# A recurrent mixer computed inside its own input product, with its small matmuls on 128 rows

## The chip, the cores and the metric

The kernel runs on one core of one Trainium2 chip (trn2). The metric is the device time of one launch in microseconds (us); the time given for a kernel is the median of its runs.

## The reference, cut to what matters

Two transformer blocks run one after the other over 256 tokens of width 1024, in float32; the first adds 16 meta tokens in front (272 columns). The first layer of the first block, the one the change is about, is a gated linear recurrence ("hgrn2") between a normalisation and an output product:

```python
hn = rmsnorm(h, g[0])
q, f_pre, i, g = split(hn @ w_in, 4)            # w_in: 1024 x 4096
f = lb + (1 - lb) * sigmoid(f_pre); logf = log(f); k = 1 - f      # 8 heads of 128
# per head, in chunks: the 16 meta tokens, then 4 chunks of 64
b = cumsum(logf); q_in = q*exp(b); k_in = k*exp(-b); k_out = k*exp(b_last - b)
o = tril(q_in @ k_in.T) @ v + q_in @ S          # S: state at the chunk's start
S = exp(b_last) * S + k_out.T @ v
o = rmsnorm_per_head(o) * head_gain * silu(g);  mix = o @ w_out
```

After it come its feed-forward layer, an attention layer ("fox") with its own, and the second block: a gated delta rule, a feed-forward layer, a latent attention ("mla") and a feed-forward layer. The second block scales, shifts and gates with `mod = silu(c) @ ada_w + ada_b`, 96 columns of 128 values, which depends on no token.

## The kernel before, in words

Activations lie feature-major: 8 tiles of 128 features by 272 (or 256) columns. Every weight product is computed to float32 precision with three fp32r matmuls per 128x128 block: high part of w by high part of x, high by low, low by high (L355 to L357). Weights stream through one ring of four slots. An item is normally 16 blocks (1 MB, two output tiles of eight blocks each, 48 matmuls). SP loads it into `raw` seven items ahead, once a slot is free. ACT copies it to `w_hi` (`split_hi`, L210), and DVE takes `w_lo` = raw - w_hi (`split_lo`, L214), three items ahead of PE. `STREAM` is the order of the items, `each` and `steps` the loops over them. ACT takes the finished tiles out of PSUM. The stages lie in blocks (`run`, `nc.Block`); at the end of each the engines wait for each other.

Some products are hosts of the modulation: beside an item, SP loads 1 MB of `ada` into a room of two slots (`mod_load`, L190), and DVE multiplies by the row `c_row` and sums (`mod_column`, L196, two of them, then L203). `MOD_HOSTS` says which product takes how many of the 48 modulation items, and `modulation_scales` turns the scales of a layer into gains in a block of its own once they are complete.

The first layer goes so. (1) Entry (`NormEntry`): ACT squares (L505), PE sums over features (L580), ACT takes the root (L509), DVE inverts (L530), scales (L567) and makes the low half (L545), ACT the high half (L519). After its entry ACT splits items 1 and 2 and applies Silu to `c_row` (L806). (2) Product `a_in`: 16 items in the order q, f, v, g of 4 items each, copied to `qfig` (L824). It hosts 8 modulation items, one at every second item. (3) `hgrn2`, in a block of its own. ACT and DVE first prepare all heads: the lower bounds `lb`, Sigmoid on f (L1425), f and k (L1485, L1488), Ln (L1428), scans (L1493). Then they go head by head (L1432 to L1437 on ACT, L1499 to L1511 on DVE). PE starts when the first head's k_out is there. Per head it has 6 transposes (L1542, L1543), 3 scores (L1545, two instructions each, as every float32 matmul here), 4 additions to the state (L1554 for the 16 meta rows, L1557 with 64 rows each), and for the head before, the output: 3 matmuls with the masked scores (L1525) and 4 with the states (L1529). Between them ACT copies the transposes (L1417, L1418) and takes the output out (L1412), and DVE masks the scores (L1452, L1454) and steps the state (L1460, L1464). (4) Product `a_out`, whose entry (`HeadNormEntry`) starts with squares on ACT (L605) after the block's end.

The attention layer of the same block (`Fox`) already has the form of a product with the heads woven in: its tile matmuls are L981 to L983, its head matmuls L998 to L1043.

Of the kernel before, what the change touches and what calls it, by code (L numbers as in the profile page):

```python
# [23 lines left out]
P = 128  # L24
# [36 lines left out]
STREAM = ([("a_in", 16, 16), ("a_out", 4, 16), ("up0", 22, 16), ("down0", 16, 11)]  # L61
# [8 lines left out]
for _g in range(4):  # L70
    SOURCE |= {f"fox_q{_g}": ("b_q", _g), f"fox_k{_g}": ("kv", _g), f"fox_v{_g}": ("kv", 4 + _g)}
# [3 lines left out]
for _name, _n, _every in (("a_in", 16, 2), ("a_out", 4, 1), ("down0", 16, 2), ("b_out", 4, 1),  # L75
                          ("down1", 16, 2), ("gdn_gate", 4, 1), ("dn0", 16, 2), ("mla_out", 4, 1)):
    MOD_HOSTS[_name] = (_at, _every)
    _at += _n // _every
# [20 lines left out]
def fused_model(nc, w, params_d, consts_d, hT_d, c_d, pos_d, out_d):  # L99
    with ExitStack() as ctx:  # L100
# [132 lines left out]
        class Product:  # L233
# [3 lines left out]
            def __init__(self, name, tiles, k_tiles, x_hi, x_lo, cols, act_out=None, dve_out=None, pool_out=None,  # L237
# [11 lines left out]
                hosts = n // every if every else 0  # L249
# [8 lines left out]
                def mod_at(s, turn):  # L258

                    slot = (s - first) % SLOTS // every % 2  # L260
                    i = turn * (SLOTS // every) + (s - first) // every
                    turns = turn * (SLOTS // every // 2) + (s - first - every * slot) // (2 * every)
                    return i + mod_first, slot, turns + turns0[slot]

                def sync(sp):
# [16 lines left out]
                    if first == 0:  # L282
                        for r in range(SLOTS, ahead):
                            load(sp, name, r, r % SLOTS)
# [371 lines left out]
        with nc.Block() as block:  # L656
            @block.sync
            def _(sp):
# [3 lines left out]
                for r in range(LEAD):  # L662
                    load(sp, "a_in", r, r % SLOTS)
                sp.dma_start(c_row[:, :], c_d).then_inc(c_in.sem, 16)
                load(sp, "a_in", LEAD, LEAD)
# [13 lines left out]
        def modulation_scales(layer):  # L679

            with nc.Block() as block:
                @block.vector
                def _(dve):
                    for part, gains in ((1, "norm_mix"), (4, "norm_ffn")):
                        dve.scalar_tensor_tensor(mod[:, layer, part, :], mod[:, layer, part, :], 1.0,
                                                 par(gains, layer * KD, KD), ALU.add, ALU.mult)
# [107 lines left out]
        with ExitStack() as outer:  # L794
            qfig = sbuf(outer, "qfig", [P, 4 * KD, T1])
            with ExitStack() as phase:
                x_hi, x_lo = sbuf(phase, "x_hi_a", [P, KD, T1], F32R), sbuf(phase, "x_lo_a", [P, KD, T1], F32R)

                def first_high(act):
                    split_hi(act, 0, 0, 0, starts["a_in"][2])  # L800

                def high_then(act):
                    for r in range(1, LEAD):
                        split_hi(act, r, r, 0, starts["a_in"][2])
                    act.wait_ge(c_in.sem, 16)
                    act.activation(c_row[:, :], c_row[:, :], ACT.Silu).then_inc(c_ready.sem, 1)  # L806

                def first_low(dve):
                    dve.wait_ge(params_in.sem, 16)
                    split_lo(dve, 0, 0, 0, starts["a_in"][2])  # L810

                def low_then(dve):
                    for r in range(1, LEAD):
                        split_lo(dve, r, r, 0, starts["a_in"][2])
                    dve.wait_ge(c_ready.sem, 1)
# [3 lines left out]
                def a_in_out(act, j, s, where):  # L819
                    item_ready(act, "a_in", j)  # L820
                    for t in range(2):
                        at = j * 2 + t
                        d = qfig[:, at, :] if isinstance(at, int) else qfig[:, bass.ds(at, 1), :]
                        last = act.activation(d, where(t)[:, 0:T1], ACT.Copy)  # L824
                    last.then_inc(item_out.sem, 1)
                product("a_in", 2, KD, x_hi, x_lo, (0, T1), act_out=a_in_out, entry=entry)

            q, f, v, g = (qfig[:, i * KD:(i + 1) * KD, :] for i in range(4))
            hgrn2(nc, sbuf, sig, bank, q, f, v, g, work, par, con, ident)
# [444 lines left out]
        modulation_scales(0)  # L1274
# [27 lines left out]
        modulation_scales(1)  # L1302


        with ExitStack() as outer:
# [33 lines left out]
            with ExitStack() as phase:  # L1339
# [3 lines left out]
                        entry=entry, sqrt_next=True)  # L1343
        ffn_layer(1, real, modcol(1, 4), "gu1", "dn1", (modcol(1, 2), False), 0, shift=modcol(1, 3))
# [24 lines left out]


def hgrn2(nc, sbuf, sig, bank, q, f, v, g, k, par, con, ident):

    real = (META, T1)
    tiles = [(0, META), (META, P), (META + P, P)]
    n_chunks = SEQ // 64
    with ExitStack() as scope:
        b = sbuf(scope, "log_decay", [P, HEADS, T1])
        e = sbuf(scope, "decay", [P, HEADS, T1])  # L1380
        k_in = sbuf(scope, "k_in", [P, HEADS, T1])
        lb = sbuf(scope, "lower_bound", [P, 6, KD])
        lb_max, lb_exp, lb_done = sig("lb_max"), sig("lb_exp"), sig("lb_done")
        sigmoided, silued = sig("f_sigmoided"), sig("g_silued")
        f_made, k_made, logged, summed = sig("f_made"), sig("k_made"), sig("f_logged"), sig("b_summed")
        exped, q_in, k_in_made, diffed = sig("b_exped"), sig("q_in"), sig("k_in_made"), sig("b_diffed")
        diff_exped = sig("diff_exped")
        reset = con("reset_hgrn")
        v_tok = sbuf(scope, "v_tok_a", [P, 2, 3, P])
        k_tok = sbuf(scope, "k_tok_a", [P, 2, 3, P])  # L1390
        attn = sbuf(scope, "attn_a", [P, 2, 3, P])
        state = sbuf(scope, "state_a", [P, 2, n_chunks, P])
        turned, copied, masked = sig("turned"), sig("tok_copied"), sig("attn_masked")
        ds_done, stated, o_done, o_out = sig("ds_done"), sig("stated"), sig("o_done"), sig("o_out")

        def added_to(y, c):


            return bank[y][:, 3 * P:4 * P] if c == 2 else bank[6][:, c * P:(c + 1) * P]

        k_out_made = sig("k_out_made")
        behind = 4

        with nc.Block() as block:
            @block.scalar
            def _(act):
                def take_out(i):
                    if i >= 2:  # L1410
                        act.wait_ge(o_done.sem, o_done.at(i - 1))
                        act.activation(v[:, i - 2, :], bank[7][:, 0:T1], ACT.Copy).then_inc(o_out.sem, 1)  # L1412
                    if i < HEADS:
                        y = i % 2
                        act.wait_ge(turned.sem, turned.at(i + 1))
                        for src, dst in ((bank[2 + y], v_tok), (bank[4 + y], k_tok)):
                            act.activation(dst[0:META, y, 0, :], src[0:META, 0:P], ACT.Copy)  # L1417
                            last = act.activation(dst[:, y, 1:3, :],  # L1418
                                                  src[:, P:3 * P].rearrange("p (x c) -> p x c", x=2), ACT.Copy)
                        last.then_inc(copied.sem, 1)  # L1420

                act.wait_ge(lb_max.sem, lb_max.at(3))
# [924 lines left out]
```

## Time and profile before

| | us |
|---|---|
| median of 3 runs | 1754.86 |
| lowest and highest run | 1753.28, 1766.72 |
| the profiled execution | 1766.81 |
| its span (first to last instruction) | 1765.0 |
| busy in the span: PE / DVE / ACT / POOL | 1554.9 / 1020.3 / 803.8 / 221.0 |
| mean granted TensorE clock | 0.912 |

A granted clock of 1.00 is 2.4 GHz and 0.50 is 1.2 GHz. A duration of a PE instruction holds its passage through the array and overlaps with the next one's; the pace is read from one start to the next. A row of the timeline gives start, length, engine, line, operation, output and inputs, and in brackets how long the engine sat idle before it and what released it. A row of the windows gives the busy time and the number of instructions of each engine in a stretch, then the granted clock, the share of the DMA engines and GB/s.

### The profile page before, as it was taken

The numbers are of one execution on the slowest core, as the hardware profiler recorded it, in microseconds if no ns is written. First come the engines' busy times: TensorE is split into PE (matmuls) and PEld (weight loads), VectorE is DVE, ScalarE is ACT, GpSimd is POOL, SyncE is SP. The second block draws the span as 40 slices with busy tenths as digits, with TensorE's granted clock in tenths as the row PEclk, the third lists the DMA queues.
The fourth block names the chain that finished last, engine by engine and source line by source line (L and its number), as shares of the span: only waits on it lengthen the run. The fifth ranks groups of instructions, "written<-read, shape, count | busy, mean of one in ns | idle before, by whom it ended". The sixth has DMA issues, their size and how long they took to land. (4 is left out here: it accounts for less than half of the span.)

```text
span 1765.0 us, 29368 instructions
## 1 busy us (share of the span) xinstructions
PE 1554.9 (88%) x11429; PEld 1475.3 (84%) x11429; DVE 1020.3 (58%) x1663; ACT 803.8 (46%) x1372; POOL 221.0 (13%) x341
## 2 busy tenths in 40 slices
PE   6976879999887998999979768979999677989997
PEld 5975678999876777999969758979999576779997
DVE  5565176776765447777778652245447634664443
ACT  5453354544454453555445472364434434543332
POOL 0000101211044320112000006211210000001200
PEclk9995599999998898999989987989999786889999
DMA  8840142548622233455925700024549332335451
GB/s 331 306 174 1 41 151 96 177 151 302 241 98 95 71 113 127 167 190 197 352 97 189 252 22 1 1 96 144 187 142 355 123 108 95 149 125 182 159 167 54
DMA packets 41134, 265.97 MB, mean 151 GB/s; under 512 B 4560, under 2 KB 5712, under 8 KB 15312
## 3 DMA queue, kind: packets, MB, share of 16 engines
q1 hardware_dynamic: 41040, 264.72, 41.8%
q8 instruction: 59, 0.97, 0.2%
q14 instruction: 35, 0.29, 0.0%
HBM read 263.65 MB, written 1.05 MB: 150 GB/s over the span
## 5 line engine op out<-in xcount | busy, mean ns | idle before, releaser
L214 DVE TENSOR_TENSOR w_lo<-raw,w_hi 128x2048 fp32r<-128x2048 f32 (+3 forms) x224 | 466.1, 2083 | 289.2 <-ACT w_hi L210 286.6
L210 ACT ACTIVATE w_hi<-raw 128x2048 fp32r<-128x2048 f32 (+3 forms) x224 | 387.6, 1732 | 56.5 <-PE bank L357 50.9
L355 PE MATMUL bank<-x_hi_up,w_hi 128*128 128x272 f32 (+1 forms) x704 | 203.7, 289 | 8.2 <-DVE x_lo_up L545 8.1
L355 PE MATMUL bank<-x_hi_gu,w_hi 128*128 128x256 f32 x704 | 202.0, 287 | 8.5 <-DVE x_lo_gu L543 8.4
L357 PE MATMUL bank<-x_hi_up,w_lo 128*128 128x272 f32 (+1 forms) x704 | 202.2, 287 | 0.0
L356 PE MATMUL bank<-x_lo_up,w_hi 128*128 128x272 f32 (+1 forms) x704 | 201.7, 287 | 0.0
L356 PE MATMUL bank<-x_lo_gu,w_hi 128*128 128x256 f32 x704 | 200.8, 285 | 0.0
L357 PE MATMUL bank<-x_hi_gu,w_lo 128*128 128x256 f32 x704 | 199.0, 283 | 0.0
L355 PEld LDWEIGHTS bank<-x_hi_gu,w_hi 128*128 128x128 f32 x704 | 133.8, 190 | 10.4 <-issue 8.9
L355 PEld LDWEIGHTS bank<-x_hi_up,w_hi 128*128 128x128 f32 x704 | 133.7, 190 | 9.9 <-issue 8.8
L357 PEld LDWEIGHTS bank<-x_hi_gu,w_lo 128*128 128x128 f32 x704 | 135.5, 192 | 0.0
L356 PEld LDWEIGHTS bank<-x_lo_gu,w_hi 128*128 128x128 f32 x704 | 134.6, 191 | 0.0
L356 PEld LDWEIGHTS bank<-x_lo_up,w_hi 128*128 128x128 f32 x704 | 134.1, 191 | 0.0
L357 PEld LDWEIGHTS bank<-x_hi_up,w_lo 128*128 128x128 f32 x704 | 133.9, 190 | 0.0
L355 PE MATMUL bank<-a_hi_up,w_hi 128*128 128x272 f32 (+1 forms) x352 | 102.8, 292 | 0.0
L580 PE MATMUL bank<-work,constants 128*128 128x256 f32 (+2 forms) x154 | 54.5, 525 | 52.8 <-ACT work L505 52.7
L357 PE MATMUL bank<-a_hi_up,w_lo 128*128 128x272 f32 (+1 forms) x352 | 100.2, 285 | 0.0
L356 PE MATMUL bank<-a_lo_up,w_hi 128*128 128x272 f32 (+1 forms) x352 | 100.1, 284 | 0.0
L356 PE MATMUL bank<-a_lo_gu,w_hi 128*128 128x256 f32 x352 | 98.3, 279 | 0.0
L355 PE MATMUL bank<-a_hi_gu,w_hi 128*128 128x256 f32 x352 | 98.3, 279 | 0.0
L357 PE MATMUL bank<-a_hi_gu,w_lo 128*128 128x256 f32 x352 | 98.3, 279 | 0.0
L580 PEld LDWEIGHTS bank<-work,constants 128*128 128x128 f32 x154 | 39.3, 265 | 66.0 <-ACT work L505 57.6
(393 smaller groups left out, 3942.2 us busy)
## 6 DMA issues: line engine op xcount, KB each, us to landing
raw<-w_up SPq DMA_DIRECT2D x44, 1024.0 KB, 4.9
raw<-w_gu SPq DMA_DIRECT2D x44, 1024.0 KB, 4.9
raw<-w_down SPq DMA_DIRECT2D x32, 704.0 KB, 5.3
raw<-w_dn SPq DMA_DIRECT2D x32, 704.0 KB, 4.1
raw<-w_a_in SPq DMA_DIRECT2D x16, 1024.0 KB, 6.8
mod_w_down<-w_ada SPq DMA_DIRECT2D x16, 1024.0 KB, 7.1
raw<-w_gdn_qkv SPq DMA_DIRECT2D x12, 1024.0 KB, 5.0
mod_w_a_in<-w_ada SPq DMA_DIRECT2D x8, 1024.0 KB, 6.5
```

What stands on the lines that cost most here:

```text
L210: act.activation(w_hi[:, s, 0:blocks * P], raw[:, s, 0:blocks * P], ACT.Copy).then_inc(hi_split.sem, 1)
L214: dve.tensor_tensor(w_lo[:, s, 0:blocks * P], raw[:, s, 0:blocks * P], w_hi[:, s, 0:blocks * P].bitcast(F32), ALU.subtract).then_inc(lo_sp ...
L355: pe.matmul(o, w_hi[:, s, b], x_hi[:, xk, cols[0]:cols[1]], start=begin, stop=False)
L356: pe.matmul(o, w_hi[:, s, b], x_lo[:, xk, cols[0]:cols[1]], start=False, stop=False)
L357: last = pe.matmul(o, w_lo[:, s, b], x_hi[:, xk, cols[0]:cols[1]], start=False, stop=end)
L580: last = pe.matmul(bank[6][:, 0:c1 - c0], ones, work[:, k, c0:c1], start=k == 0, stop=k == n - 1)
```

## The change

`hgrn2` and product `a_in` become one class, `Hgrn`, run in one block with an order written out by hand:

- The items of `a_in` come in the order f0 to f3, then q0 v0 q1 v1 q2 v2 q3 v3, then g0 to g3. Tiles alternate between banks 0 and 1, and `half_done` and `copied_out` count single tiles.
- The lower bounds are made ahead of the entry (ACT's Exp ahead of the squares). ACT splits items 1, 2 and 3 after the entry, and not `c_row`, whose Silu moves behind the heads.
- Order: 8 tiles of f (ACT applies Sigmoid as it takes them out, DVE makes f and k), all logarithms, 2 tiles of q, then twelve steps `head(i)`, each followed by one item (two tiles) for i from 0 to 10. In `head(i)` PE makes the output of head i-4, transposes and scores of head i-2, and the additions to the state of head i-3.
- The scratch tiles `b`, `e`, `k_in` hold 3 heads in place of 8; chunk decays are kept in a small tile. Transposed keys go into four tiles of 128 rows of which the rest is zero, and the meta rows of v and of the scores are padded with zeros to 128 rows. POOL clears them once. So L1554 and L1557 become 4 matmuls of 128 rows, and the meta matmul of L1525 contracts over 128 rows.
- Modulation: `a_in` hosts none; `gdn_out` (4), `mla_in` (1) and `uq` (3) become hosts. `modulation_scales(1)` is split in two, with a further block after `mla_out`.

```diff
-STREAM = ([("a_in", 16, 16), ("a_out", 4, 16), ...
+A_ITEMS = [f"a_f{g}" for g in range(4)] + [f"a_{x}{g}" for g in range(4) for x in "qv"] + [f"a_g{g}" for g in range(4)]
+STREAM = ([(name, 1, 16) for name in A_ITEMS] + [("a_out", 4, 16), ...
-for _name, _n, _every in (("a_in", 16, 2), ("a_out", 4, 1), ("down0", 16, 2), ("b_out", 4, 1),
-                          ("down1", 16, 2), ("gdn_gate", 4, 1), ("dn0", 16, 2), ("mla_out", 4, 1)):
+for _name, _n, _every in (("a_out", 4, 1), ("down0", 16, 2), ("b_out", 4, 1), ("down1", 16, 2), ("gdn_gate", 4, 1),
+                          ("gdn_out", 4, 1), ("dn0", 16, 2), ("mla_in", 3, 4), ("uq", 3, 1), ("mla_out", 4, 1)):
...
+                order = [tile("f", n) for n in range(KD)] + [("logs", "", 0), tile("q", 0), tile("q", 1)]
+                items = [(x, m) for m in range(4) for x in "qv"][1:] + [("g", m) for m in range(4)]
+                for i in range(HEADS + 4):
+                    order.append(("head", "", i))
+                    if i < len(items):
+                        x, m = items[i]
+                        order += [tile(x, 2 * m), tile(x, 2 * m + 1)]
+                    if i == HEADS:
+                        order.append(("gates", "", 0))
...
+                    def product_tile(event):
+                        r, t = ring_of(event), event[2] % 2
+                        s, m = r % SLOTS, turn[event]
+                        if t == 0:
+                            pe.wait_ge(lo_split.sem, r + 1)
+                        if m >= 2:
+                            tile_taken(pe, in_turn[m - 2])
...
+                        if 2 <= i < HEADS + 2:
+                            j, y = i - 2, i % 2
+                            tile_taken(pe, tile("v", j))
+                            pe.wait_ge(q_in.sem, q_in.at(j + 1))
+                            pe.wait_ge(k_in_made.sem, k_in_made.at(j + 1))
+                            pe.wait_ge(k_out_made.sem, k_out_made.at(j + 1))
...
+                            for c in range(n_chunks):
+                                last = pe.matmul(bank[6][:, c * P:(c + 1) * P], k_tok[:, y, c, :],
+                                                 v_tok[:, y, (c + 1) // 2, :], start=True, stop=True)
...
+                def gpsimd(pool):
+                    pool.memset(k_tok[:, :, :, :], 0.0)
+                    pool.memset(v_tok[:, :, 0, :], 0.0)
+                    pool.memset(attn[:, :, 0, :], 0.0).then_inc(cleared.sem, 1)
...
-        modulation_scales(1)
+        modulation_scales(1, [(1, "norm_mix")])
...
+        modulation_scales(1, [(4, "norm_ffn")])
```

On DVE, `head(i)` does in this order: the state of head i-3, the mask of head i-2, the scan of head i+1, q_in and k_out of head i-1, then the chunk decays, k_in and the differences of head i; `split_lo` of the item four further on comes after each second tile. On ACT it is: two Exps of head i, the Exp for k_out of head i-1, the output of head i-4, the five copies of head i-2; then the two tiles and `split_hi`.

## Rows read from the trace of the kernel before

**Rows 1.** Windows: product `a_in`, preparation, head by head, entry of `a_out`.

```profile
22.75:122.00 99.25, 99.20 (x768) 98.74 (x768) 65.39 (x71) 47.63 (x57) 0.00 (x0) 0.97 0.72 264
122.00:139.70 17.70, 0.00 (x0) 0.00 (x0) 12.64 (x41) 14.88 (x33) 0.00 (x0) 0.64 0.13 53
139.70:213.60 73.90, 61.14 (x272) 51.76 (x272) 25.01 (x79) 18.34 (x57) 0.00 (x0) 0.52 0.00 1
213.60:225.50 11.90, 5.87 (x16) 4.27 (x16) 1.75 (x5) 11.53 (x27) 5.79 (x8) 0.76 0.45 177
```

**Rows 2.** Timeline of PE: one head of `hgrn2`, clock 0.50.

```profile
165.99 1.72 PE L1525 MATMUL bank<-attn_a,v_tok_a 16*128 16x16 f32 x6 [1.58 <-issue]
...
169.11 0.42 PE L1542 MATMUL bank<-constants,qfig 128*16 128x128 f32 x1
...
170.52 1.39 PE L1545 MATMUL bank<-qfig,k_in 128*16 128x16 f32 x6
171.84 0.79 PE L1554 MATMUL bank<-v_tok_a,k_tok_a 16*128 16x128 f32 x2
...
175.37 1.73 PE L1525 MATMUL bank<-attn_a,v_tok_a 16*128 16x16 f32 x6 [1.58 <-issue]
```

**Rows 3.** Timeline of ACT: last output of `hgrn2`, then the entry of `a_out`.

```profile
213.63 0.40 ACT L1412 ACTIVATE qfig<-bank 128x272 f32<-128x272 f32 x1 [5.84 <-PE bank L1529]
...
214.86 2.67 ACT L605 ACTIVATE qfig<-qfig 128x272 f32<-128x272 f32 x8 [0.28 <-PEq L1406]
```

**Rows 4.** Timeline of ACT: after the entry of `a_in`, and the logarithms.

```profile
27.21 3.70 ACT L210 ACTIVATE w_hi<-raw 128x2048 fp32r<-128x2048 f32 x2
30.93 1.28 ACT L806 ACT_TABLE_LOAD   x1
...
129.75 2.67 ACT L1428 ACTIVATE qfig<-qfig 128x272 f32<-128x272 f32 x8
```

**Rows 5.** Timeline of DVE: first splits of `a_in`.

```profile
29.14 4.50 DVE L214 TENSOR_TENSOR w_lo<-raw,w_hi 128x2048 fp32r<-128x2048 f32 x2 [1.36 <-ACT w_hi L210]
```

**Rows 6.** Timeline of PE: `a_in` starts after a gap.

```profile
22.75 0.56 PE L355 MATMUL bank<-x_hi_a,w_hi 128*128 128x272 f32 x1 [4.03 <-DVE x_lo_a L545]
...
28.50 0.29 PE L355 MATMUL bank<-x_hi_a,w_hi 128*128 128x272 f32 x1
```

**Rows 7.** Timeline of PE: delta rule, float32 matmuls at clock 1.00.

```profile
1110.46 1.92 PE L2035 MATMUL bank<-constants,inverse 128*128 128x128 f32 x16
1112.22 3.68 PE L2022 MATMUL bank<-inverse,coupling_level 128*128 128x64 f32 x32
```

**Rows 8.** Windows: three of the woven attention, one of the delta rule.

```profile
602.00:604.00 2.00, 1.01 (x9) 0.79 (x7) 2.00 (x8) 0.00 (x0) 1.81 (x4) 1.00 0.36 61
...
606.00:608.00 2.00, 2.00 (x10) 1.30 (x10) 1.31 (x6) 0.23 (x1) 0.16 (x1) 0.50 0.35 147
...
612.00:614.00 2.00, 2.00 (x18) 2.00 (x17) 0.00 (x0) 0.00 (x0) 0.00 (x0) 1.00 0.00 0
...
1078.00:1080.00 2.00, 2.00 (x11) 2.00 (x11) 0.42 (x1) 0.00 (x0) 0.00 (x0) 0.50 0.00 0
```

**Rows 9.** Timeline of DVE: end of `uq`, end of `gdn_out`, last item of `mla_out`.

```profile
1446.85 1.23 DVE L214 TENSOR_TENSOR w_lo<-raw,w_hi 128x1024 fp32r<-128x1024 f32 x1 [3.04 <-ACT w_hi L210]
...
1179.17 2.29 DVE L214 TENSOR_TENSOR w_lo<-raw,w_hi 128x2048 fp32r<-128x2048 f32 x1 [3.41 <-ACT w_hi L210]
1183.35 3.26 DVE L557 SCALAR_TENSOR_TENSOR h<-work,mod,h 128x256 f32<-128x256 f32 x8 [1.88 <-PEq L398]
...
1546.08 1.22 DVE L196 CUSTOM_DVE_ANT_0 mod_w_mla_out<-mod_w_mla_out,c_row 128x1024 f32<-128x1024 f32 x1
...
1548.96 3.25 DVE L557 SCALAR_TENSOR_TENSOR h<-work,mod,h 128x256 f32<-128x256 f32 x8 [0.31 <-PEq L398]
```

**Rows 10.** Timeline of ACT: first instruction after `uq`.

```profile
1450.42 0.72 ACT L505 ACTIVATE work<-latent 128x256 f32<-128x256 f32 x2 [0.28 <-PEq L398]
```

More of the change, by code:

```diff
@@ L58 @@
 NCONST = _at
-STREAM = ([("a_in", 16, 16), ("a_out", 4, 16), ("up0", 22, 16), ("down0", 16, 11)]
+A_ITEMS = [f"a_f{g}" for g in range(4)] + [f"a_{x}{g}" for g in range(4) for x in "qv"] + [f"a_g{g}" for g in range(4)]
+STREAM = ([(name, 1, 16) for name in A_ITEMS] + [("a_out", 4, 16), ("up0", 22, 16), ("down0", 16, 11)]
           + [(f"fox_q{g}", 1, 16) for g in range(4)] + [("fox_gate", 1, 8)]
@@ L248, in __init__ @@
                 mod_first, every = MOD_HOSTS.get(name, (0, 0))
-                hosts = n // every if every else 0
+                hosts = -(-n // every) if every else 0
                 ahead = LEAD + SLOTS
@@ L258, in mod_at @@
                 def mod_at(s, turn):
+                    if hosts == 1:
+                        return mod_first, 0, turns0[0]
                     slot = (s - first) % SLOTS // every % 2
@@ L281, in sync @@
                         mod_load(sp, room, mod_first + i, i)
-                    if first == 0:
-                        for r in range(SLOTS, ahead):
-                            load(sp, name, r, r % SLOTS)
                     cut = max(first, first + n - ahead)
@@ L662, in _ @@
                 for r in range(LEAD):
-                    load(sp, "a_in", r, r % SLOTS)
+                    load(sp, A_ITEMS[r], r, r % SLOTS)
                 sp.dma_start(c_row[:, :], c_d).then_inc(c_in.sem, 16)
-                load(sp, "a_in", LEAD, LEAD)
+                load(sp, A_ITEMS[LEAD], LEAD, LEAD)
             @block.vector
@@ L677, in _, with modulation_scales @@
                 pe.wait_ge(consts_in.sem, 16)
-        def modulation_scales(layer):
+        def modulation_scales(layer, parts):
             with nc.Block() as block:
@@ L683, in _ @@
                 def _(dve):
-                    for part, gains in ((1, "norm_mix"), (4, "norm_ffn")):
+                    for part, gains in parts:
                         dve.scalar_tensor_tensor(mod[:, layer, part, :], mod[:, layer, part, :], 1.0,
@@ L794, in fused_model @@
         with ExitStack() as outer:
             qfig = sbuf(outer, "qfig", [P, 4 * KD, T1])
+            q, f, v, g = (qfig[:, i * KD:(i + 1) * KD, :] for i in range(4))
             with ExitStack() as phase:
                 x_hi, x_lo = sbuf(phase, "x_hi_a", [P, KD, T1], F32R), sbuf(phase, "x_lo_a", [P, KD, T1], F32R)
[L799 to L815, printed above, removed]
-                entry = NormEntry(lambda k: h[:, k, :], KD, (0, T1), gain1(0, 0), x_hi, x_lo, act_first=first_high,
-                                  dve_first=first_low, act_then=high_then, dve_then=low_then)
@@ L819, in a_in_out @@
[L819 to L828, printed above, removed]
@@ L829, in fused_model @@
-            hgrn2(nc, sbuf, sig, bank, q, f, v, g, work, par, con, ident)
+                run(Hgrn(phase, x_hi, x_lo, q, f, v, g))
             with ExitStack() as phase:
```

439 lines of the change are left out of this document (257 added, 182 removed).

## The prediction, as it was written before the run

> **What bounds the kernel now.** I read the windows by stage first, then the timelines of PE, ACT and DVE inside the first layer, then the clock of other stages. In product `a_in` PE is busy 99.20 of 99.25 us [rows 1]: PE is the bound, DVE has 34 us and ACT 52 us to spare. In the next 17.7 us PE does nothing while ACT and DVE prepare the heads. Then come 73.9 us of heads in which PE is busy 61.1, but at a clock of 0.52, that is nearly always at 1.2 GHz [rows 1]. One head takes 175.37 - 165.99 = 9.38 us, of which PE waits 1.58 for the states and works 7.80 [rows 2]. So 91.6 us pass between the product and the end of the heads (122.0 to 213.6) whose work for PE, at full clock, is small. The entry of `a_out` starts with squares at 214.86 [rows 3]; this moment is what I compare.
>
> **PE's work per head at full clock.** The trace shows no such head. In the delta rule float32 instructions of the same kind run at 1.00: 16 with 128 columns in 1112.22 - 1110.46 = 1.76 us, 0.11 each, and 32 with 64 columns in about 3.5 (3.68 less the 0.2 in which the last one ends), 0.11 too [rows 7]. A head after the change has 6 transposes (0.66), 4 score instructions of 128 columns and 2 small ones (0.5), 8 for the state (0.88), 6 for the masked scores (0.66) and 8 for the output from the states (0.88): 3.6 us. The other way, half of the 7.80 measured at 1.2 GHz is 3.9. I take 3.85, as switches between operands and semaphores come on top of the 3.6. Ends: 3.6 (-2 us over 8 heads) and 7.8, if the heads ran at 1.2 GHz (+32 us).
>
> **Padding.** It changes 8 instructions of the state's additions and 2 of the output. At 1.2 GHz the two of L1554 take 0.79 us with only 16 rows; two of 128 rows would take 0.22 and 0.42, the length of the transpose at 169.11 [rows 2], so fewer rows buy no time. I take nothing. Ends: 8 x 8 x 0.11 = 7 us gained or lost if an instruction of part rows cost double or were free. The zeroing by POOL runs at the start, where POOL has no other work, and its first reader comes some 50 us later. The Trainium skill (TensorE: Matmul & The Clock Gate, Part 3, packing small matmuls) says that matmuls in different row groups run side by side; that speaks against padding, since L1557's 64-row pieces alternate between two halves. By it the padding costs at most half of 6 x 0.11 us a head, 2.6 us in all. The measured 0.79 us for the two 16-row ones shows that at least those gained nothing.
>
> **The start of the new block.** The lower bounds and their Exp come ahead of the squares: +0.2 us. PE's first tile is done at 28.50 + 0.2 [rows 6], the second at 31.75. The third needs bank 0, which ACT takes only after three splits. ACT ends x_hi at 27.2, splits until 27.4 + 5.5 = 32.9 (3.70 for two, [rows 4]), loads the Sigmoid table (1.28, as at L806), takes tile 0 at 34.2 to 34.6. DVE's splits (4.50 for two, [rows 5]) are ready before. So PE idles 2.9 us, where it now idles none, and may restart at 1.2 GHz. After the 4.03 us gap at 22.75 the first 24 matmuls took 28.50 - 22.75 = 5.75 us, against (122.0 - 28.5) / 31 = 3.02 us for each later tile [rows 1, 6]. The same after 2.9 us costs up to 2.7; I take 1.5. Six more tiles of f: 34.65 + 1.5 + 18.1 = 54.2. PE goes on with the two tiles of q until 60.2. ACT meanwhile takes f7 (54.6), splits (56.5), loads a table and makes the 8 logarithms (1.28 + 2.67, [rows 4]: 60.5), and takes q0 at 60.85. PE waits 0.7 and starts v0 at 60.9; v0 and v1 end at 66.9.
>
> **The woven part.** From there PE has 10 items (20 x 3.02 = 60.3) and 8 heads (8 x 3.85 = 30.8): 158.0, then ACT's copy of the last output (0.40) and the block's end (0.28, both [rows 3]): squares at 158.7. The wait of 1.58 per head goes, since the states have a whole item's time to be made. What is late next? One period is 6.04 + 3.85 = 9.9 us. DVE's head work is (12.64 + 25.01) / 8 = 4.7 us and ACT's, tables included, (14.88 + 18.34) / 8 = 4.2 [rows 1]; the splits add 2.3 and 1.9, the copies of two tiles 0.7 on ACT. DVE is busy 7.0 and ACT 6.8 of 9.9. The tightest order is DVE's: after the second tile's end ACT copies and splits (2.3), DVE makes w_lo (2.3), then the head: states, mask, scan, q_in, k_out, about 3.5; k_out is out 8.1 us after the tile, and PE reads it at 9.9 plus the output matmuls. Nothing is late by this, with 1.8 us to spare. For hand-overs that come out less well, twelve of them, I add 2 us. Saved in the stage: 214.86 - 158.7 - 2 = 54 us.
>
> In `a_in` DVE loses 8 modulation items and SP their loads (8 MB of DMA). DVE was no bound there, so this gains nothing. The ring's loads go through the same seven-item lead; an item has 10 us in the weave where it had 6.
>
> **The modulation's new hosts.** `gdn_out`: the last `split_lo` begins at 1179.17, the next stage's DVE work at 1183.35, 4.18 later. In `mla_out`, a host, the last `mod_column` runs from 1546.08 and the next stage starts at 1548.96, 2.88 later, to which the split's 2.2 is added: 5.1 [rows 9]. So +0.9. `uq`: last split at 1446.85, ACT goes on at 1450.42 [rows 9, 10]; with 1.2 + 2.88 it would be 1450.95: +0.5. `mla_in` has its column beside the first item, where DVE waits for ACT: nothing. The further block: one small operation between two barriers of 0.3: +0.6. Sum +2; ends 0 and 6, if a modulation item lands late in `uq` (three items in 16 us, where SP must issue the third after the first is used).
>
> **Sum.** -54 + 2 = -52 us. The profiled execution took 1766.81, 1.81 more than its span, so it becomes 1715. It is the slowest of the three runs; 52 us off the median give 1754.86 - 52 = 1703.
>
> **Rivals.** (A) The clock falls at every head. For it: 61 us of float32 work at 0.52 [rows 1], and a window of the delta rule with PE busy 2.00 of 2.00 at 0.50 [rows 8], so busy float32 matmuls do not by themselves bring 2.4 GHz. Against it: in the woven attention the clock stood at 1.00 over a window with PE only half busy, fell to 0.50 in the next four us, and was back at 1.00 by 612, after a few us of tile matmuls [rows 8]. Price: 3.9 more per head and 1.6 on the tiles behind it, 8 x 5.5 = 44 us: 1747. The Trainium skill (the same page, Part 4, transposes) says that transposes do not count as work for the clock gate; by it A gains weight. The heads' rows at 0.52 agree with it, but each head here has only 0.66 us of transposes between 6 us of products.
>
> (B) The hand-overs, not PE, set the period: DVE, last in the ring from `split_hi` over `split_lo` to k_out, has 1.8 us to spare, and decides from there on. If a period is 12 instead of 9.9 us, 8 x 2.1 = 17 us: 1720. For it: both engines work in strict order, with five waits on DVE per head. Against it: their busy sums of 7 us.
>
> (C) The slower side: the clock stays at 1.2 GHz from the first head on, since head work stands in each stretch. Then 60.3 + 30.8 us take twice as long, +91: 1794. It decides if the tiles between two heads do not bring the clock back. Against it: `a_in` regained 2.4 GHz at 28.5 after 5.75 us of them [rows 6].
>
> (D) The padding doesn't do what it is there for, and changes nothing. That moves no number above.
>
> **How the numbers follow.** My forecast 0.80, B 0.11, A 0.06, C 0.03. A measurement of this kernel tells about 1% (17.5 us) from no change. Forecast and B are faster by more: 0.91; A lies within: 0.06; C is slower: 0.03. The range: down to 1690 (3.6 per head, no slow restart, late hand-overs none, and runs that differ by 13 us), up to 1726 (B, or the clock falling at three heads in ten).
>
> **What would show it.** The first squares of `a_out`'s entry near 159 to 162; the clock 0.9 or more in the weave; no matmul row with 64 or 16 rows in it; PE's gap of about 3 us after its second tile and 0.7 us before v0; head groups of 3.9 us between pairs of 3.0 us tiles; `gdn_out` and `uq` ending about 1 us later. I am wrong if PE's waits in the weave add up to over 10 us, or if head groups take 7 us.

## The result, and the profile after

| | before | after |
|---|---|---|
| median (lowest to highest), runs | 1754.45 us (1753.28 to 1766.72), 4 | 1714.07 us (1712.86 to 1715.16), 4 |
| profiled execution: time, span | 1766.81, 1765.0 | 1712.86, 1711.0 |
| TensorE clock over the span | 0.912 | 0.928 |
| first squares of the entry of `a_out` | 214.86 | 159.44 |
| first product matmul of `mla_out` | 1524.0 | 1470.7 |

The ratio is 0.9759 (95% interval 0.972 to 0.9799): 40.4 us off the median, where the forecast was 52 off (1703). The range (1690 to 1726) holds it. Profile against profile the gain is 1766.81 - 1712.86 = 53.95. So the two comparisons differ by 13.5 us, and explaining that is most of what follows.

First the stage that was changed. The windows of the kernel after (from the first product tiles on; columns as in [rows 1]):

```profile
22.00:28.00 6.00, 5.94 (x29) 5.14 (x29) 4.72 (x13) 4.20 (x7) 0.00 (x0) 0.72 0.17 68
28.00:32.00 4.00, 2.57 (x21) 2.34 (x19) 3.77 (x2) 3.98 (x4) 0.00 (x0) 1.00 0.15 18
32.00:40.00 8.00, 6.36 (x28) 6.39 (x29) 6.50 (x8) 3.97 (x5) 0.00 (x0) 0.57 0.99 389
40.00:50.00 10.00, 10.00 (x82) 10.00 (x81) 4.99 (x9) 3.88 (x5) 0.00 (x0) 1.00 0.40 147
60.00:70.00 10.00, 9.36 (x75) 9.17 (x74) 3.89 (x7) 7.98 (x13) 0.00 (x0) 1.00 0.60 211
100.00:110.00 10.00, 10.00 (x87) 9.78 (x85) 6.10 (x14) 5.08 (x13) 0.00 (x0) 1.00 0.30 107
150.00:158.00 8.00, 8.00 (x69) 8.00 (x68) 3.54 (x5) 2.06 (x4) 0.00 (x0) 1.00 0.38 131
```

Where [rows 1] had 17.7 us without PE and then 73.9 us at a clock of 0.52, PE is now busy nearly all the time, and at a clock of 1.00 from 40 us to the end of the block. The exceptions are the two that were forecast: one gap with a restart (28 to 40), and one wait of 0.64 us ahead of the first tile of v, at 61.34. Behind that PE waits for nothing until the squares.

One head in the woven order, timeline of PE (start, us, engine, line, operation, tiles, count). Up to 109.14 the tile matmuls of the item before it run; from 112.90 those of the next:

```profile
109.14 0.83 PE L894 MATMUL bank<-attn_a,v_tok_a 128*128 128x16 f32 x6
109.81 1.00 PE L898 MATMUL bank<-qfig,state_a 128*128 128x64 f32 x8
110.65 0.49 PE L912 MATMUL bank<-constants,qfig 128*16 128x128 f32 x3
110.98 0.49 PE L914 MATMUL bank<-constants,qfig 128*16 128x128 f32 x3
111.40 0.86 PE L916 MATMUL bank<-qfig,k_in 128*16 128x16 f32 x6
112.09 1.06 PE L925 MATMUL bank<-v_tok_a,k_tok_a 128*128 128x128 f32 x8
112.90 0.38 PE L881 MATMUL bank<-x_hi_a,w_hi 128*128 128x272 f32 x1
...
119.01 0.83 PE L894 MATMUL bank<-attn_a,v_tok_a 128*128 128x16 f32 x6
```

The six lines answer to [rows 2]. They take 112.90 - 109.14 = 3.76 us where a head took 7.80 and a wait of 1.58. Not one of them waits for another engine, and the period is 119.01 - 109.14 = 9.87 us.

The two places where the change costs something, timelines of ACT and PE after the entry of `a_in` (the bracket is the idle time and what ended it), and the end of the stage on ACT, which answers to [rows 3]:

```profile
26.29 5.50 ACT L212 ACTIVATE w_hi<-raw 128x2048 fp32r<-128x2048 f32 x3
31.81 1.28 ACT L1065 ACT_TABLE_LOAD   x1
33.10 0.69 ACT L1065 ACTIVATE qfig<-bank 128x272 f32<-128x272 f32 x2
...
158.75 0.40 ACT L1039 ACTIVATE qfig<-bank 128x272 f32<-128x272 f32 x1 [1.11 <-PE bank L898]
159.44 2.67 ACT L606 ACTIVATE qfig<-qfig 128x272 f32<-128x272 f32 x8 [0.28 <-PEq L399]
```
```profile
33.65 0.56 PE L881 MATMUL bank<-x_hi_a,w_hi 128*128 128x272 f32 x1 [3.08 <-ACT qfig L1065]
```

PE's third tile waits for ACT, which first finishes three splits (5.50) and a table load (1.28). The gap is 3.08 us. After it the first 26 matmuls take 39.67 - 33.65 = 6.02 us, and at 0.125 each they would have taken 3.25: the restart costs 2.8 in this profile. The cost isn't the same in every profile, as the part on the prediction shows.

The stage ends 214.86 - 159.44 = 55.4 us earlier. The rest of the kernel gives 1.5 of that back up to the end, by the two profiles. But one stage of it, the latent attention (scores at L1335 and L1336 before, L1611 and L1612 after), does not stand still, as the experiments show.

### The profile page after: what moved, and what is told of

Read it like the earlier page. It is cut to its first block and busy times, and to the rows that moved or that the text cites. A ratio compares the mean times of both kernels' runs of the same rounds, so it can differ in the third digit from the quotient of the medians.

```text
span 1711.0 us, 29323 instructions
## 1 busy us (share of the span) xinstructions
PE 1527.9 (89%) x11429; PEld 1456.7 (85%) x11429; DVE 1019.8 (60%) x1671; ACT 798.1 (47%) x1367; POOL 222.3 (13%) x344
## 3 DMA queue, kind: packets, MB, share of 16 engines
HBM read 263.65 MB, written 1.05 MB: 155 GB/s over the span
```

## The experiments

Three questions were open: what the two other parts of the change (new hosts, padding) do alone, why before has two groups of times, and which of them the profile of before belongs to. Of the 55 later runs of before, beside which the experiments were measured in three batches, 50 lie at 1752 to 1757 us and 5 at 1767 to 1769: 4 of the 23 in the first batch, 1 of the 23 in the second, none of the 9 in the third. The first batch ran beside the first four experiments, the second beside the four with padded scores or the early take, the third beside the last three; each was on another chip of the same type.

**The kernel before once more.**

> The kernel before, unchanged, for a second profile. The profiled executions differ by 54 us (1766.8 to 1712.9), the medians by 40. Theory: the first profiled execution was slow in the head-by-head stretch, where the clock stood at 0.52; in the others part of it runs at 2.4 GHz. Then this profile takes about 1754, its entry of a_out starts with squares near 203 instead of 214.9, and the clock of the heads is 0.6 or more. Rival: that stretch is the same (squares at 214 to 215, clock 0.52) and the 13 us lie in later stages, which differ from run to run.

Measured: 1755.42. My theory put the difference into the heads; it fell. The squares are at 211.78 (214.86 in the first profile), so the heads were 3.1 us shorter, but most of the 11.4 us between the two profiles isn't there: the later stages level that out (the first matmul of the latent attention's stage starts at 1473.7 in the one and 1474.5 in the other), and then `mla_out` starts at 1524.0 and at 1513.8. Between the two points lies the latent attention. Its scores, with 128 rows (L1335) and 64 rows (L1336), in the profile given for the kernel before (duration in ns least/median/most, then first to last start):

```profile
L1335 PE MATMUL bank<-k_nope,q_mla x32: 275/452/793, 1485.2 to 1515.9; 128*128 128x128 f32 x16, 128*128 128x256 f32 x16
L1336 PE MATMUL bank<-latent,q_mla x32: 272/530/793, 1485.9 to 1516.5; 64*128 64x128 f32 x16, 64*128 64x256 f32 x16
```

The same two lines of the same kernel in this run:

```profile
L1335 PE MATMUL bank<-k_nope,q_mla x32: 275/378/483, 1485.7 to 1505.7; 128*128 128x128 f32 x16, 128*128 128x256 f32 x16
L1336 PE MATMUL bank<-latent,q_mla x32: 272/374/480, 1486.1 to 1506.3; 64*128 64x128 f32 x16, 64*128 64x256 f32 x16
```

One kernel, two courses: 31 us of scores with matmuls of up to 0.79 us, or 20 us with at most 0.48. The window of four us in the middle of it, in the first profile of before and in this one:

```profile
1492.00:1496.00 4.00, 4.00 (x10) 2.01 (x9) 1.77 (x8) 0.91 (x4) 0.00 (x0) 0.50 0.00 0
```
```profile
1492.00:1496.00 4.00, 4.00 (x23) 2.77 (x22) 3.10 (x15) 1.51 (x8) 0.00 (x0) 1.00 0.00 0
```

PE is busy 4.00 of 4.00 in both, once at 0.50 with 10 matmuls, once at 1.00 with 23. The profile from which I predicted is of the longer course; the median of before is of the shorter one. And after? Its own lines:

```profile
L1611 PE MATMUL bank<-k_nope,q_mla x32: 275/421/793, 1433.6 to 1462.6; 128*128 128x128 f32 x16, 128*128 128x256 f32 x16
L1612 PE MATMUL bank<-latent,q_mla x32: 272/480/792, 1434.0 to 1463.2; 64*128 64x128 f32 x16, 64*128 64x256 f32 x16
```

After has the longer course (29 us of scores) in its profile, and its other three runs lie within 2.3 us of that one; that they ran the same course is read from their times.

**Only the new hosts**, with `a_in` and `hgrn2` as before:

```diff
-for _name, _n, _every in (("a_in", 16, 2), ("a_out", 4, 1), ...
+for _name, _n, _every in (("a_out", 4, 1), ... ("gdn_out", 4, 1), ("dn0", 16, 2), ("mla_in", 3, 4), ("uq", 3, 1), ...
...
-                hosts = n // every if every else 0
+                hosts = -(-n // every) if every else 0
...
-        modulation_scales(1)
+        modulation_scales(1, [(1, "norm_mix")])
...
+        modulation_scales(1, [(4, "norm_ffn")])
```

> The kernel before with only the modulation moved: a_in hosts none, gdn_out, mla_in and uq do, and the gains of the second layer's feed-forward are made in a further block. My sum says +2 us (0.9 in gdn_out, 0.5 in uq, 0.6 for the block). Rival: the eight items in a_in did hold DVE or the loads back, then it is faster than before by some us; or a late item in uq, then +4 to +6.

Measured: 1766.97 (1757.9 to 1770.99, 12 runs), ratio 1.0055 (1.0032 to 1.0079). That is 12.7 more than before, and 11 of the 12 runs lie at 1764 to 1771. The profile has the scores from 1486.5 to 1517.8, again with up to 0.79 us for one. So the small rearrangement of DVE's work seems to take the attention to its longer course in nearly every run (by their times; one run has a profile). What it costs by itself is measured further down.

**Only the padding**, in the unwoven `hgrn2`:

```diff
-        k_tok = sbuf(scope, "k_tok_a", [P, 2, 3, P])
+        k_tok = sbuf(scope, "k_tok_a", [P, 2, n_chunks, P])
...
-                            pe.matmul(bank[7][:, t0:t0 + n], v_tok[0:n, y, x, :], attn[0:n, y, x, 0:n],
+                            pe.matmul(bank[7][:, t0:t0 + n], v_tok[:, y, x, :], attn[:, y, x, 0:n],
...
-                            last = pe.matmul(added_to(y, c + 1), k_tok[r, y, 1 + c // 2, :],
-                                             v_tok[r, y, 1 + c // 2, :], start=True, stop=True)
+                            last = pe.matmul(added_to(y, c), k_tok[:, y, c, :],
+                                             v_tok[:, y, (c + 1) // 2, :], start=True, stop=True)
```

> The kernel before with only the padding: transposed keys, meta values and meta scores on 128 rows in the unwoven heads. My theory: padding alone changes nothing (+-3 us), the heads stay near 0.52 and 9.4 us each. Rival: the matmuls of 16 and 64 rows are what keeps the clock at 1.2 GHz in the heads; then the heads run at 2.4 GHz, 5.5 us each in place of 9.4, and the kernel is some 20 to 30 us faster.

Measured: 1741.82 (1732.98 to 1752.78, 12 runs), ratio 0.9933 (0.9904 to 0.9963), 12.5 less than before, and the squares at 198.73 in place of 211.78. My expectation that the padding changes nothing falls. The runs scatter: two lie at 1733 to 1737, five at 1740 to 1742, five at 1750 to 1753, so 12.5 is the middle of gains from about 2 to 21. Most of the gain in the profile is in the clock. First the heads of before (second profile), then the same stretch and parts of it in this kernel:

```profile
139.70:198.00 58.30, 48.77 (x234) 41.33 (x233) 22.13 (x71) 16.82 (x55) 0.00 (x0) 0.59 0.00 1
```
```profile
139.70:198.00 58.30, 45.08 (x272) 40.29 (x270) 24.70 (x79) 21.33 (x67) 0.00 (x0) 0.73 0.00 1
144.00:153.50 9.50, 6.29 (x54) 5.75 (x54) 7.61 (x25) 4.94 (x18) 0.00 (x0) 1.00 0.01 2
154.30:155.72 1.42, 1.42 (x8) 1.01 (x8) 0.19 (x1) 0.40 (x1) 0.00 (x0) 0.50 0.00 0
161.00:173.50 12.50, 10.92 (x51) 9.76 (x52) 2.26 (x8) 2.45 (x8) 0.00 (x0) 0.50 0.00 1
```

The five profiles with unpadded heads have 0.53 to 0.59 over this stretch, this one 0.73. In both kinds the clock goes up and down; without the padding it is at 1.00 in one to three short stretches, with it in two long ones and two short ones. Which instruction raises it isn't shown: in the padded kernel it also stays at 0.50 through a whole head (161 to 173.5), and without the padding, in the second profile of before, it rises between 160.5 and 161.0, over transposes and before the additions (161.72). (The Trainium skill, TensorE: Matmul & The Clock Gate, Part 4, says that transposes do not count for the clock as other matmuls do. This trace doesn't decide it: the clock has fallen already when the six transposes at 154.30 begin (0.85 from 153.5 to 154.0), while the six at 148.42 run at 1.00; in the weave the same six transposes per head stand between product tiles and the clock stays at 1.00.)

**The weave without the padding.** The first hunk undoes the padding of the keys; the meta matmuls get their 16 rows back the same way. With it go one more semaphore wait ahead of the additions, a third addition into another bank, and one copy less on ACT:

```diff
-                            for c in range(n_chunks):
-                                last = pe.matmul(bank[6][:, c * P:(c + 1) * P], k_tok[:, y, c, :],
-                                                 v_tok[:, y, (c + 1) // 2, :], start=True, stop=True)
+                            pe.wait_ge(masked.sem, masked.at(j + 1))
+                            pe.matmul(added_to(y, 0), k_tok[0:META, y, 0, :], v_tok[0:META, y, 0, :], start=True, stop=True)
+                            for c in range(n_chunks - 1):
+                                r = slice(64 * (c % 2), 64 * (c % 2) + 64)
+                                last = pe.matmul(added_to(y, c + 1), k_tok[r, y, 1 + c // 2, :],
+                                                 v_tok[r, y, 1 + c // 2, :], start=True, stop=True)
```

> The kernel after without the padding: additions to the state with 16 and 64 rows, the third of them in another bank, the meta scores and values with 16 rows, no zeroing. My theory: as the kernel after, 1714 +-3 us, clock 1.00 in the weave. Rival: part rows let the clock fall at each head; then the weave is up to 44 us longer and the kernel is near the one before.

Measured: 1718.09 (1715.55 to 1720.38, 6 runs), 4.0 more than after. The clock over 100 to 120 us is 1.00, so here it isn't the clock. Timeline of PE, one head and the start of the next:

```profile
109.53 0.29 PE L886 MATMUL bank<-x_hi_a,w_lo 128*128 128x272 f32 x1
109.75 1.03 PE L897 MATMUL bank<-attn_a,v_tok_a 16*128 16x16 f32 x6
110.62 1.00 PE L901 MATMUL bank<-qfig,state_a 128*128 128x64 f32 x8
...
112.99 0.48 PE L928 MATMUL bank<-v_tok_a,k_tok_a 16*128 16x128 f32 x2
113.41 0.71 PE L931 MATMUL bank<-v_tok_a,k_tok_a 64*128 64x128 f32 x6
114.04 0.39 PE L884 MATMUL bank<-x_hi_a,w_hi 128*128 128x272 f32 x1
...
120.25 1.03 PE L897 MATMUL bank<-attn_a,v_tok_a 16*128 16x16 f32 x6
```

The period is 10.50 in place of 9.87. The outputs from masked scores, whose first product (of three) has 16 rows, take 110.62 - 109.75 = 0.87 (0.67 with 128 rows), and start 0.22 after the last tile matmul in place of 0.12. That place costs 0.20 + 0.10 = 0.30. The additions take 114.04 - 112.99 = 1.05 (0.81) and start 0.78 after the scores' last line (0.69, that line being the same in both): 0.24 + 0.09 = 0.33. Together that is the 0.63, at full clock, and 8 x 0.63 = 5.0 us in all. The squares are only 4.0 us later than in the kernel after (163.40), since the restart behind PE's gap was cheaper here by 1.4. Of the 0.33 a part may belong to the added wait or the other bank; for the 0.30 there is a run with nothing else changed (the last one below). The Trainium skill has a rule for either side. TensorE: Matmul & The Clock Gate, Part 3, has matmuls in different row groups run side by side; the eight instructions of the additions take longer with part rows here, not less. The Trainium skill's page TensorEngine Tiling (Array Packing), Tiling Modes, Key Properties, says "Changing tiling mode (not just tile) drains the TensorE"; the rows fit that, with 0.30 to 0.33 us for each such place.

**The attention's short scores padded too.** If matmuls of part rows keep the clock down, padding the 64-row scores of the latent attention (L1612) must bring the shorter course for good. The edit, on the kernel after:

```diff
-                    return pe.matmul(out, q_rope[p0:p0 + 64, h_ // 2, q0:q0 + qn], k_rope[p0:p0 + 64, 0, 0:kn],
+                    return pe.matmul(out, q_rope[:, h_ // 2, q0:q0 + qn], k_pad[:, h_ % 2, 0:kn],
...
+                        for y in range(2):
+                            r = slice(64 * y, 64 * y + 64)
+                            last = dve.tensor_tensor(k_pad[r, y, :], x[r, t, :], other[r, i, :], ALU.add)
...
+                pool.memset(k_pad[64:P, 0, :], 0.0)
+                pool.memset(k_pad[0:64, 1, :], 0.0).then_inc(zeroed.sem, 1)
```

> The kernel after, and besides the rotated keys of the latent attention (64 rows per head, in two halves of one tile) in two tiles of 128 rows, the other half zero, so that its logits have no matmul of 64 rows. Theory: that attention has two ways to run, 32 us with the clock at 1.00 and 43 us with it at 0.50; the median of before holds the first, the kernel after always the second, and the part rows are what lets the clock stay low. Then this kernel takes 1714 - 11 = 1703, first logits to the entry of mla_out in 32 us or less. Rival: rows do not matter, only the moment at which the stage begins; then it stays at 1714 or takes either value at random.

Measured: 1700.44 (1699.18 to 1702.06, 5 runs), ratio 0.9685 (0.9659 to 0.9712), 13.6 less than after. The lines of the two scores:

```profile
L1611 PE MATMUL bank<-k_nope,q_mla x32: 273/378/382, 1434.0 to 1450.5; 128*128 128x128 f32 x16, 128*128 128x256 f32 x16
L1612 PE MATMUL bank<-k_rope_padded,q_mla x32: 275/327/379, 1434.3 to 1450.9; 128*128 128x128 f32 x16, 128*128 128x256 f32 x16
```

The scores start 0.3 to 0.4 us later than in the kernel after (1434.0 against 1433.6), and end 12.3 us earlier (1450.9 against 1463.2); no matmul is over 0.38 us.

**The same edit on the kernel before:**

> The kernel before with the same padding of the rotated keys. Theory: its runs near 1767 (4 of 23) go, the rest stays within 2 us of 1753. Rival: no change in how often the slow value comes.

Measured: 1751.79 (1748.91 to 1754.14, 12 runs), ratio 0.9979 (0.9964 to 0.9994). None of the 12 runs is in the upper group, but with only 1 of 23 runs of before there in the same batch, this alone shows little. The scores now take 16.6 us (1486.1 to 1502.7) where the unpadded ones took 20.2 in the second profile of before (1486.1 to 1506.3), whose clock was at 1.00 from 1488 on: an estimate of 3.6 us for what the padding is worth here without a change of course.

**The same edit on the kernel with only the new hosts:**

> The moved modulation alone (as e2, which took 1767) with the padded rotated keys. Theory: the 13 us that e2 lost are 11 of the attention's clock and 2 of the hosts themselves; so this is 2 us above e6. Rival: the hosts cost 10 us or more by themselves (DVE or DMA), then it stays near 1765.

Measured: 1754.38 (1753.08 to 1758.8, 11 runs), ratio 1.0001 (0.9986 to 1.0016). The 12.7 us of the hosts shrink to 1754.38 - 1751.79 = 2.6. That is their own price; the other 10 were the attention's clock. The two hosts kernels ran on different chips, but that isn't the cause: the next kernel, with unpadded scores and on the same chip as this one, has the longer course. And with the attention in one course on both sides, the whole change is 1700.44 - 1751.79 = -51.4 us.

**The third tile's wait.** On the kernel after, ACT takes the first tile out before it splits item 2, and the second before it splits item 3:

```diff
-                    for r in range(1, LEAD + 1):
-                        split_hi(act, r, r, 0, 16)
+                    split_hi(act, 1, 1, 0, 16)
...
+                            if turn[event] < 2:
+                                split_hi(act, n + 2, n + 2, 0, 16)
```

> The kernel after with ACT taking the first tile of f ahead of its splits of items 2 and 3. In the profile of after PE idled 3.1 us there and then ran 6 us at 1.2 GHz. Theory: both go, 3.1 + 2.9 = 6 us, squares of a_out's entry at 153.5. Rival: the restart at 1.2 GHz comes anyway, at another place, then 3 us.

Measured: 1708.2 (1705.61 to 1710.96, 5 runs), ratio 0.9726 (0.9699 to 0.9753), 5.9 less than after. The windows show neither gap nor restart:

```profile
22.00:30.00 8.00, 7.48 (x40) 7.33 (x41) 6.50 (x15) 5.81 (x9) 0.00 (x0) 0.65 0.15 56
30.00:34.00 4.00, 4.00 (x33) 3.79 (x32) 2.77 (x2) 3.99 (x5) 0.00 (x0) 1.00 0.45 125
```

The squares come at 154.30, 5.1 earlier. The gap and the restart had cost 3.1 + 2.8 = 5.9 in the profile of after; PE's first matmul comes 0.7 us later here (22.52 against 21.84). The two profiles as wholes differ by 1.9 us only (1710.96 and 1712.86), because this one has the scores of the attention for 31.3 us (1430.1 to 1461.4) where that of after had 29.6.

**Both edits together.**

> The kernel after with both: padded rotated keys (e5: 1700.4) and the early taking of the first tile of f (e8: 6 us). Theory: they lie in different stages and add: 1694 to 1695. Rival: the moved start puts the attention or another stage at a bad moment for the clock; then 1700 or more.

Measured: 1696.86 (1694.73 to 1697.88, 5 runs), ratio 0.9666 (0.9653 to 0.9679), the fastest kernel here. Over the padded attention alone the early take gives 3.6 us. The squares are 3.9 earlier than there (154.75 against 158.67), where they were 5.1 earlier without the padding. The difference fits the restart: it had cost 2.9 in the profile of after and 1.6 in that of the kernel with the padded attention, so there was less to win.

**The modulation column ahead of the split**, in the last item of a host (on top of both edits), so that the stage's end doesn't wait for the column:

```diff
+                        column_first = host and isinstance(r, int) and r == first + n - 1
+                        if column_first:
+                            mod_column(dve, room, *mod_at(s, turn))
...
```

> As e9, and in the last item of each host with a modulation column per item DVE makes the column ahead of the split. Theory: DVE's end of a_out, b_out, gdn_gate, gdn_out, uq and mla_out comes up to 1 us earlier each, 3 to 5 us in all: 1690. Rival: PE or ACT ends these stages anyway, or the later split is late at the next entry; then no change (+-1 us) against e9.

Measured: 1699.4 (1698.18 to 1702.16, 5 runs), 2.5 slower than without. DVE's timeline at the end of `gdn_out` shows one cause:

```profile
1123.12 1.23 DVE L198 CUSTOM_DVE_ANT_0 mod_w_gdn_out<-mod_w_gdn_out,c_row 128x1024 f32<-128x1024 f32 x1 [2.66 <-DMA mod_w_gdn_out<-w_ada]
...
1125.62 2.28 DVE L216 TENSOR_TENSOR w_lo<-raw,w_hi 128x2048 fp32r<-128x2048 f32 x1
```

The column's weights had not landed, DVE waited 2.66 us for them with `w_lo` queued behind, and `w_lo` (1125.62) came 2.1 us later than in the kernel without the edit (1123.56). So DVE went on to the next stage at 1128.70 (1128.64 without the edit), although this one had begun 1.3 earlier. `mla_out` has the same wait, with 2.0 us. Behind the split, in the kernel without the edit, neither stage waits for its columns' data. Further differences of about one us, in stages whose columns did not wait, are not explained.

**The meta rows unpadded again**, with the attention padded, in the output's one product only:

```diff
-                                pe.matmul(bank[7][:, t0:t0 + n], v_tok[:, y, x, :], attn[:, y, x, 0:n], start=x == 0,
+                                pe.matmul(bank[7][:, t0:t0 + n], v_tok[0:n, y, x, :], attn[0:n, y, x, 0:n], start=x == 0,
```

> As e5, but the output's meta matmul again with 16 rows; the additions to the state keep 128. In the profiles the six masked-score instructions take 0.66 us from start to start with 128 rows and 0.87 with 16, the whole period 9.87 against 10.50 without any padding. Theory: each change between full and part rows costs time by itself, at the full clock too: 8 x 0.2 = 1.7 us here, and 3.4 from the state's. So 1702. Rival: the difference of 4 us between e4 and after is the clock's or the moment's, then no change or a jump of 10 us.

Measured: 1703.88 (1701.64 to 1704.43, 5 runs), 3.4 more than with it padded. Timeline of PE:

```profile
106.86 1.03 PE L894 MATMUL bank<-attn_a,v_tok_a 16*128 16x16 f32 x6
107.72 1.00 PE L898 MATMUL bank<-qfig,state_a 128*128 128x64 f32 x8
...
117.00 1.03 PE L894 MATMUL bank<-attn_a,v_tok_a 16*128 16x16 f32 x6
```

The period is 10.14, and 0.27 us of it come from one 16-row product, 8 x 0.27 = 2.2 in all. The theory had 0.2 and 1.7. The profiled run is the fastest of the five (1701.64) and doesn't show the whole 3.4: its squares are at 158.81, only 0.1 later than with the product padded, because PE's gap ended 0.7 us earlier here and the restart behind it cost 1.5 less. The rest of the 3.4 is not traced. The attention may hold some of it: in this profile some scores take up to 0.64 us, the clock is 0.50 from 1432 to 1436, and the scores end at 1452.1, 30.9 us after the first matmul of the stage, where the kernel with all padded needed 28.8. So padding the short scores makes the shorter course far likelier; it doesn't rule every fall of the clock out.

## Why the prediction was right, and where it was off

**PE's work per head at full clock (3.85).** Right: 3.76 for the group and 9.87 for a period of 9.9.

**The start of the new block.** The gap was 3.08 (forecast 2.9). The restart cost 2.8 where I took 1.5, with 2.7 as the upper end. That doesn't make the upper end the right row: four profiles have this gap, of 3.08 or 3.09 us, and the clock behind it went four ways. The windows behind it in the kernel after and in the one with the 16-row product:

```profile
34.00:42.00 8.00, 8.00 (x44) 8.00 (x44) 5.12 (x8) 1.98 (x2) 0.00 (x0) 0.64 1.01 399
```
```profile
34.00:42.00 8.00, 8.00 (x66) 8.00 (x65) 5.60 (x11) 3.99 (x4) 0.00 (x0) 1.00 0.99 380
```

From the end of the gap to the next wait PE has eight tiles, 24.16 us at 3.02 each. They took 27.05 in the kernel after, 25.63 in the weave without padding, 25.79 with the padded attention and 24.28 with the 16-row product: by this reckoning the restart cost 2.9, 1.5, 1.6 and 0.1 (2.8 was the count over the first 26 matmuls alone). So a term of 1.5 was a fair middle of what this gap costs, and any single run may be 1.4 off either way.

**Woven part.** The first tile of v was to start at 60.9 and starts at 61.34. From there to the squares the sum has 158.7 - 60.9 = 97.8 us, and 159.44 - 61.34 = 98.1 were measured, so of the 2 us for hand-overs 0.3 were needed. Rival B did not come: PE waits for no engine in this whole stretch.

**Rivals A and C.** The clock is 1.00 from 40 us on. Between product tiles the heads run at it, although the same heads alone ran at 0.52.

**Padding.** "I take nothing" failed, and so did rival D. At full clock the padding is worth 0.63 us a head, 5.0 in all (4.0 by the medians of the two kernels), and in the unwoven stage, clock included, 12.5 us. The row on which I relied, 0.79 us for the two 16-row instructions against 0.42 for one of 128 rows [rows 2], already said that part rows cost as much as full ones or more; I read it as "no gain" and didn't ask whether there is a price for the change of rows. The sum wasn't harmed, since 3.85 had been made from instructions of 128 rows.

**The new hosts (+2).** Their own price is 2.6 (with the padded scores on both sides), and the ends lie about where forecast. DVE's timeline of after, at the end of `gdn_out`, of `uq`, and at the further block:

```profile
1128.19 2.29 DVE L216 TENSOR_TENSOR w_lo<-raw,w_hi 128x2048 fp32r<-128x2048 f32 x1 [0.93 <-ACT w_hi L212]
...
1133.28 0.88 DVE L558 SCALAR_TENSOR_TENSOR h<-work,mod,h 128x256 f32<-128x256 f32 x2 [0.30 <-PEq L399]
...
1396.19 1.23 DVE L216 TENSOR_TENSOR w_lo<-raw,w_hi 128x1024 fp32r<-128x1024 f32 x1 [0.56 <-ACT w_hi L212]
...
1495.69 0.17 DVE L686 SCALAR_TENSOR_TENSOR mod<-mod,feature_params 128x8 f32<-128x8 f32 x1 [0.30 <-PEq L399]
```

From the last split to the next stage `gdn_out` now takes 1133.28 - 1128.19 = 5.09 us (4.18 in [rows 9]; +0.9 as forecast). After `uq` ACT goes on at 1400.19, 4.00 after the split, where it was 3.57 [rows 9, 10]: +0.4 for a forecast of +0.5. The block costs 0.5.

**The sum: the step that failed.** "It is the slowest of the three runs; 52 us off the median give 1703." The saving was worked out against a profiled execution of one course of the latent attention and taken off a median of the other. Between the profiles it holds: -52 forecast, -54 measured. With the attention fixed in its shorter course on both sides it holds too: -51.4. Between the medians it gives only -40.4, since the kernel after, unlike most runs of before, has the longer course. Of the 11.4 us between the two profiles of before 11.0 lie in the latent attention's stage, which takes 1524.0 - 1473.7 = 50.3 us in one and 1513.8 - 1474.5 = 39.3 in the other, from its first matmul to that of `mla_out`; in the kernel after it takes 1470.7 - 1422.0 = 48.7. The new hosts alone brought the longer course in 11 of 12 runs, so they are the likely cause in the kernel after too; the weave without them was not run. That the profile was 12 us above the median of its own kernel was written down in the prediction and passed over. It asked for an explanation: some stage was able to take 10 us more or less with the same instructions, and any change might move it. The mechanism of the weave was right; that 1714 lies in the range although the forecast was 11 us off is owed to the width of the range (36 us), not to a term that foresaw this.

What stays open: why the new hosts tip the attention over. Its stage starts after other DVE work and at another moment; neither was varied by itself.

## What to carry to other kernels

When a profiled execution lies near one per cent off its kernel's median, find the stage that differs before subtracting anything from the median, since the edit may move that stage from one course to the other. Look for float32 matmuls of few rows between those of 128: padding them with zero rows adds no columns, saved 0.27 to 0.33 us at each place in the heads at full clock, and more where the clock wavers (12.5 us in the unwoven heads; 13.6 in the attention, of which it would save some 3.6 at full clock too, by the estimate above). Work moved forward in an engine's own order needs its data earlier too, so look at when its DMA lands before moving it.

## What was not expected of the hardware

- In the latent attention TensorE's clock stood at 0.50 with PE busy 4.00 of 4.00 us. In the kernel before the same instructions ran at 0.50 in one profile and at 1.00 in the other. Two windows of the kernel after, the first in the middle of it, the second where the clock is back:

```profile
1452.00:1456.00 4.00, 4.00 (x13) 2.87 (x13) 1.78 (x8) 1.57 (x6) 0.00 (x0) 0.50 0.01 2
1458.00:1462.00 4.00, 4.00 (x23) 2.87 (x22) 2.71 (x14) 1.69 (x7) 0.00 (x0) 1.00 0.00 0
```

- In the kernel with the padded scores a window that is less full stands at 1.00:

```profile
1440.00:1444.00 4.00, 3.62 (x21) 2.72 (x21) 2.86 (x14) 2.87 (x11) 0.00 (x0) 1.00 0.00 0
```

- Padding matmuls of part rows changed the course of the clock. With the 64-row scores padded, none of the 11 runs of the hosts variant came over 1759, where 11 of 12 had without; for before it is none of 12 against 5 of 55. And with the additions padded the clock of the unwoven heads was 0.73 over 139.7 to 198.0, where five profiles without had 0.53 to 0.59. The edits also move the moments at which the matmuls come, and why rows should matter no run here shows.
- A gap of the same length, 3.08 or 3.09 us, was followed by tiles at a clock of 1.00 in one kernel and by about 6 us at 0.50 in another.
- One 16-row product among those of 128 rows costs 0.27 us more than the same product with 128 rows, whose two instructions take 0.22 us, at a clock of 1.00.
